# A four-layer transformer chain on one core: 22 expert slots for 20, silu written where the product goes, transposed products over the gathered x, one slot in dead tables and the gate factor

## What is computed

```python
def ec_moe(x, w_router, w_gate, w_up, w_down):
    B, N, _ = x.shape
    cap = CAPACITY_FACTOR * N // N_EXPERTS
    aff = jax.nn.softmax(jnp.einsum('bnd,de->bne', x, w_router).astype(jnp.float32), axis=-1)
    gates, idx = lax.top_k(jnp.swapaxes(aff, 1, 2), cap)
    bidx = jnp.arange(B)[:, None, None]
    xin = x[bidx, idx]
    h = jax.nn.silu(jnp.einsum('becd,edf->becf', xin, w_gate)) * jnp.einsum('becd,edf->becf', xin, w_up)
    out = jnp.einsum('becf,efd->becd', h, w_down) * gates[..., None].astype(x.dtype)
    return jnp.zeros_like(x).at[bidx, idx].add(out.astype(x.dtype))
...
    for i in range(DEPTH):
...
        x = layer_norm(ALPHA * x + h, ln_g[i, 0], ln_b[i, 0])
        y = ec_moe(x, moe_router[i], moe_w_gate[i], moe_w_up[i], moe_w_down[i])
        x = layer_norm(ALPHA * x + y, ln_g[i, 1], ln_b[i, 1])
```

## Time and profile before

| | us |
|---|---|
| median of 3 runs | 1781.36 (1778.82 to 1783.51) |
| the profiled execution | 1783.23 |
| its span on the core | 1780.7 |
| TensorE matmuls busy | 1421.6 |
| TensorE weight loads busy | 928.4 |
| VectorE busy | 601.4 |
| ScalarE busy | 428.1 |
| bytes moved | 533.48 MB, mean 300 GB/s |

### The profile page before, as it was taken

One profiled execution on the slowest core, in us unless ns is written; L12 is line 12 of the kernel. 1 busy time (PEld: TensorE's weight loads), 2 busy tenths in 40 slices (PEclk: granted clock), 3 DMA queues, 4 the chain that ended last, 5 costly groups with the idle time before them and its releaser, 6 DMA issues.

```text
span 1780.7 us, 21467 instructions
## 1 busy us (share of the span) xinstructions
PE 1421.6 (80%) x9010; PEld 928.4 (52%) x9010; DVE 601.4 (34%) x988; ACT 428.1 (24%) x671; POOL 39.3 (2%) x47
## 2 busy tenths in 40 slices
PE   7999765575575799997655755758999999999997
PEld 6788221121121475672211211215999989899996
DVE  5555100000000247651000000002555566865556
ACT  3442100000000233430000000001343454654343
POOL 3000000000000002100000000000000000000000
PEclk9989888777787889998886887869999999999999
DMA  9726999999999952379999999999546665236560
GB/s 338 219 109 273 415 423 424 424 425 423 425 423 424 389 215 95 126 283 424 423 424 424 425 424 424 424 424 386 180 166 197 229 211 166 72 99 205 178 203 24
DMA packets 148836, 533.48 MB, mean 300 GB/s; under 512 B 9868, under 2 KB 73628, under 8 KB 100508
## 3 DMA queue, kind: packets, MB, share of 16 engines
q1 hardware_dynamic: 146148, 527.07, 75.5%
q10 hardware_dynamic: 1176, 2.18, 0.8%
q0 software_dynamic: 1440, 3.18, 0.6%
HBM read 529.78 MB, written 2.62 MB: 299 GB/s over the span
## 4 chain that ended last, share of the span: by engine, by line
PE 52%; DMA 36%; DVE 5%; SPq 4%; ACT 2%; issue 1%; DVEq 0%; ACTq 0%
PE bank L1668 14%; PE bank L613 11%; DMA arena<-in_moe_w_up 9%; DMA moe_slots<-in_moe_w_up 9%; DMA xT<-in_moe_w_down 8%; PE bank L1684 7%; PE bank L1114 5%; DMA moe_slots<-in_moe_w_down 3%; DMA xT<-in_moe_w_up 3%; DMA ring<-in_moe_w_down 3%; PE bank L497 3%; PE bank L1154 3%; PE bank L314 2%; SPq L1308 2%; SPq L1300 1%; DMA ring<-in_moe_w_up 1%
## 5 line engine op out<-in xcount | busy, mean ns | idle before, releaser
L568 DVE TENSOR_TENSOR w_lo<-ring,w_hi 128x1024 fp32r<-128x1024 f32 x200 | 244.4, 1224 | 239.7 <-ACT w_hi L563 232.4
L1114 PE MATMUL bank<-ring,arena 128*32 128x512 f32 x1016 | 217.8, 738 | 99.4 <-DMA ring<-in_moe_w_up 47.9
L563 ACT ACTIVATE w_hi<-ring 128x1024 fp32r<-128x1024 f32 x200 | 211.2, 1058 | 315.9 <-PE bank L1668 151.2
L1668 PE MATMUL bank<-xT_hi,w_hi 128*128 128x256 f32 x704 | 199.8, 284 | 0.6 <-DVE xT_lo L460 0.4
L1668 PE MATMUL bank<-xT_hi,w_lo 128*128 128x256 f32 x704 | 199.2, 283 | 0.0
L1668 PE MATMUL bank<-xT_lo,w_hi 128*128 128x256 f32 x704 | 199.2, 283 | 0.0
L1154 PE MATMUL bank<-ring,arena 128*32 128x512 f32 x536 | 133.9, 815 | 79.0 <-DMA moe_slots<-in_moe_w_down 25.1
L1273 DVE TENSOR_TENSOR arena<-arena,bank 64x512 f32<-64x512 f32 x32 | 22.1, 690 | 433.1 <-ACT arena L1209 433.1
L1114 PEld LDWEIGHTS bank<-ring,arena 128*32 128x32 f32 x1016 | 46.2, 122 | 217.8 <-issue 215.7
L1668 PEld LDWEIGHTS bank<-xT_hi,w_hi 128*128 128x128 f32 x704 | 135.1, 192 | 1.6 <-issue 0.9
L1668 PEld LDWEIGHTS bank<-xT_lo,w_hi 128*128 128x128 f32 x704 | 135.1, 192 | 0.7
(11 more groups left out here) (286 smaller groups left out, 2313.9 us busy)
## 6 DMA issues: line engine op xcount, KB each, us to landing
ring<-in_moe_w_gate SPq DMA_DIRECT2D x76, 1024.0 KB, 26.5
ring<-in_moe_w_down SPq DMA_DIRECT2D x65, 1024.0 KB, 27.0
ring<-in_moe_w_up SPq DMA_DIRECT2D x51, 1024.0 KB, 26.8
arena<-in_moe_w_up SPq DMA_DIRECT2D x28, 1024.0 KB, 26.8
arena<-in_moe_w_gate SPq DMA_DIRECT2D x28, 1024.0 KB, 26.5
moe_slots<-in_moe_w_up SPq DMA_DIRECT2D x24, 1024.0 KB, 26.8
moe_slots<-in_moe_w_gate SPq DMA_DIRECT2D x24, 1024.0 KB, 26.6
moe_slots<-in_moe_w_down SPq DMA_DIRECT2D x24, 1024.0 KB, 27.1
```

The lines of the kernel that those rows point to most:

```text
L563: nc.scalar.activation(dst, raw, ACT.Copy).then_inc(hi_ready, 1)
L568: nc.vector.tensor_tensor(lo, raw, hi.bitcast(F32), ALU.subtract).then_inc(split_ready, 1)
L1114: last = nc.tensor.matmul(ps[B_GU[j % 2]][32 * c:32 * c + 32, :], xin[:, k, j * CAP:(j + 1) * CAP], w, start=(k == 0), stop=(k == KD - 1), ...
L1668: last = nc.tensor.matmul(ps[2 * s + f][:, n * SEQ:(n + 1) * SEQ], w_parts[wp][:, buf, k * P:(k + 1) * P], (xT_hi3, xT_lo3)[xp][:, k, :], ...
```

## The change

- A 21st slot (`SPARE_SLOT`) lies in the arena from column 2816. The room comes from two edits: silu is written to rows 64 to 127 of `hmid`, where the odd expert's product goes, and the tile `silu` is gone; `hT` lies over `xin`, which for that is laid out by expert first (`xin[:, j, k, :]`), so that the copy for experts 0 and 1 overwrites only their gathered x.
- ScalarE's silu of an odd expert waits for VectorE's product of the expert before it. The wait for the last group's scatter moves from VectorE's product and ScalarE's copy to ScalarE's silu of expert 0.
- A 22nd slot (`CONST_SLOT`) consists of two rows of 1024 columns, `cst` from 256 to 1279 and `gk_w`. Its units are loaded by two transfers of 512 KB. It stands behind the fourth load of a layer; it waits for mLSTM's chunk 15 in layer 0 and for GLA's gate product in layer 1. The last 22 units of a layer do without it.
- The memset and the loads of `gk_w` move on GpSimd's queue from the setup to the place between mLSTM and GLA, behind a wait for the last unit of layer 0 in the 22nd slot, and have a counter of their own (`gk_in`), for which TensorE waits ahead of the gate product.

```diff
-NSLOT = 20
+NSLOT = 22
+SPARE_SLOT, CONST_SLOT = 20, 21
...
-        for slots, u in ((ARENA_SLOTS, mixer[11]), (SPLIT_SLOTS, mixer[15]), ((XT_SLOT,), mixer[15])):
+        for slots, u in (((CONST_SLOT,), mixer[8]), ((*ARENA_SLOTS, SPARE_SLOT), mixer[11]), (SPLIT_SLOTS, mixer[15]), ((XT_SLOT,), mixer[15])):
...
-        return self.units(count, range(NSLOT))
+        return self.units(count - NSLOT, range(NSLOT)) + self.units(NSLOT, range(CONST_SLOT))
...
+        spare_at = 2816
+        slots += [arena[:, spare_at:spare_at + SLOT], None]
+        const_rows = (cst[:, C_SEL:C_SEL + D], gk_w[:, :])
...
-        xin = ar(KD * SLOTS_E).rearrange("p (k c) -> p k c", k=KD)
-        silu = ar(2 * HALF).rearrange("p (b n) -> p b n", b=2)
+        xin_hT = ar(KD * SLOTS_E)
+        xin = xin_hT.rearrange("p (j k c) -> p j k c", j=GROUP, k=KD)
+        hT = xin_hT.rearrange("p (b c) -> p b c", b=2)
...
-                                                        xin[:, k, j * CAP:(j + 1) * CAP], w, start=(k == 0),
+                                                        xin[:, j, k, :], w, start=(k == 0),
...
-                    nc.scalar.activation(silu[64:128, j % 2, :], ps[B_GU[j % 2]][0:64, :], ACT.Silu).then_inc(silu_ready, 1)
+                    if j == 0 and g:
+                        act.wait_ge(scattered, n - m)
+                    elif j % 2:
+                        act.wait_ge(h_ready, 4 * n + j)
+                    nc.scalar.activation(hmid[64:128, j // 2, :], ps[B_GU[j % 2]][0:64, :], ACT.Silu).then_inc(silu_ready, 1)
...
-                elif u.slot in ARENA_SLOTS:
+                elif u.slot == CONST_SLOT and m == 0:
+                    sp.wait_ge(const_ready, 2)
+                    sp.wait_ge(chunk_done, ml_mix.done(15))
+                elif u.slot == CONST_SLOT:
+                    sp.wait_ge(ga_psum, 1)
+                elif u.slot in ARENA_SLOTS or u.slot == SPARE_SLOT:
                     sp.wait_ge(z_ready, NT * (m + 1))
...
+            def load(u, src):
+                if u.slot == CONST_SLOT:
+                    for k in range(2):
+                        sp.dma_start(const_rows[k], src[:, k * D:(k + 1) * D]).then_inc(slot_landed[u.slot], 16)
...
             pe.wait_ge(glr_ready, 1)
+            pe.wait_ge(gk_in, 32)
...
+        def gk_gpsimd(pool, link):
+
+            pool.wait_ge(unit_done, max(u.n for u in moe_u[0] if u.slot == CONST_SLOT) + 1)
             link(nc.gpsimd.memset(gk_w[0:2 * RANK, :], 0.0))
...
             ml_gpsimd(pool)
+            gk_gpsimd(pool, link)
             gla_gpsimd(pool)
```

More of the change, by code:

```diff
@@ L132, in unit @@
         s = min(allowed, key=lambda slot: self.last.get(slot, slot - NSLOT))
-        self.landed[s] += 16
+        self.landed[s] += 32 if s == CONST_SLOT else 16
         last = self.last.get(s)
@@ L235, in program, with slot_row @@
         slots += [moe_slots[:, n * SLOT:(n + 1) * SLOT] for n in range(4)] + [xT[:, :]]
+        spare_at = 2816
+        slots += [arena[:, spare_at:spare_at + SLOT], None]
+        const_rows = (cst[:, C_SEL:C_SEL + D], gk_w[:, :])
+        def slot_row(u, k):
+            return const_rows[k] if u.slot == CONST_SLOT else slots[u.slot][:, k * D:(k + 1) * D]
         def slot(u, k):
@@ L1024, in program @@
         pick_gT = ar(NT * P)
-        assert ar.at <= arena_w - 4 * SLOT
+        assert ar.at <= spare_at and spare_at + SLOT <= arena_w - 4 * SLOT
         ar = Arena()
@@ L1203, in moe_scalar @@
                     for k in (2 * part, 2 * part + 1):
-                        ins = nc.scalar.activation(xin[:, k, :], xin_psum(k), ACT.Identity,
+                        ins = nc.scalar.activation(xin[:, :, k, :], xin_psum(k).rearrange("p (j c) -> p j c", j=GROUP), ACT.Identity,
                                                    bias=pair_col(m, 1, k), scale=pair_col(m, 0, k))
@@ L1265, in moe_vector @@
                     for k in (2 * part, 2 * part + 1):
[L1266 removed]
+                        ins = nc.vector.tensor_scalar(xin[:, :, k, :], xin_psum(k).rearrange("p (j c) -> p j c", j=GROUP), pair_col(m, 0, k), pair_col(m, 1, k),
                                                       ALU.mult, ALU.add)
@@ L1270, in moe_vector @@
                     dve.wait_ge(silu_ready, 4 * n + j + 1)
-                    if j == 0 and g:
-                        dve.wait_ge(scattered, n - m)
-                    nc.vector.tensor_tensor(hmid[64 * (j % 2):64 * (j % 2) + 64, j // 2, :], silu[64:128, j % 2, :],
+                    nc.vector.tensor_tensor(hmid[64 * (j % 2):64 * (j % 2) + 64, j // 2, :], hmid[64:128, j // 2, :],
                                             ps[B_GU[j % 2]][64:128, :], ALU.mult).then_inc(h_ready, 1)
@@ L1290, in wait_slot @@
                     sp.wait_ge(xT_taken, m + 1)
+            def load(u, src):
+                if u.slot == CONST_SLOT:
+                    for k in range(2):
+                        sp.dma_start(const_rows[k], src[:, k * D:(k + 1) * D]).then_inc(slot_landed[u.slot], 16)
+                else:
+                    sp.dma_start(slots[u.slot], src).then_inc(slot_landed[u.slot], 16)
             for g in range(NGROUP):
@@ L1299, in moe_sync @@
                             src = a[name][m, g * GROUP + j].rearrange("(q p k) f -> p q (k f)", p=P, k=2)
-                            sp.dma_start(slots[u.slot], src[:, part, :]).then_inc(slot_landed[u.slot], 16)
+                            load(u, src[:, part, :])
                 for q in range(KD // 2):
@@ L1306, in moe_sync @@
                         src = a["moe_w_down"][m, g * GROUP + j].rearrange("(q p k) d -> p q k d", p=P, k=2)
-                        cols = slice(0, HALF if tail else D)
-                        sp.dma_start(slot(u, 2)[:, :, cols], src[:, q, :, cols]).then_inc(slot_landed[u.slot], 16)
+                        if tail:
+                            sp.dma_start(slot(u, 2)[:, :, 0:HALF], src[:, q, :, 0:HALF]).then_inc(slot_landed[u.slot], 16)
+                        else:
+                            load(u, src[:, q].rearrange("p k d -> p (k d)"))
                     if tail:
```

12 lines of the change are left out of this document (5 added, 7 removed).

## The result

The changed kernel takes 1770.79 us (median of 13 runs, 1767.57 to 1776.79); the kernel before, run beside it, 1781.13 us (13 runs, 1776.14 to 1783.51). The ratio of the two is **0.9959, 95% interval 0.9947 to 0.9971**, which is 7.3 us less (5.2 to 9.4). The two medians lie 10.3 us apart, the means 7.7. The executions of the changed kernel fall into two clusters, seven from 1767.57 to 1770.79 and six from 1775.51 to 1776.79, and its median is the last of the lower one. Those of the kernel before spread from 1776.14 to 1783.51. So a median can jump by some 5 us on one execution, and the ratio with its interval is the better number. One execution of run x9 (1832.11 us) and one of x4 (2515.31) were in a slower state of the chip and stand in no ratio. The profiled execution took 1770.46 us, with a span of 1768.6.

The account below looks back on a forecast made before the run. The expert layers were taken as bound by their weight stream, 424 GB/s or 2.47 us a unit. From 1781.36 us, -9.89 for two slots and +1.1 for short rows, -8.8 in all, gave 1772.6 us, range 1769.0 to 1777.8.

Parts of the forecast that it names:

- What bounds the layers: Both expert layers: weight stream without gaps at 424 GB/s, 2.47 us a unit, from the first reuse of a slot on.
- -9.89 us for two slots: Both expert layers: 22 units instead of 20 loaded by the restart, 4.94 us less in each.
- The cover ahead of the restart: Before each layer's first slot reuse: the two extra loads fit into holes of the transfers and cost nothing.
- The price of a constants unit, +0.08: Expert streams: 14 units with 4 KB rows take 2.55 us each, +1.1 us in all; ends 0 and +5.5.
- The gate factor: GpSimd, behind unit 158 of layer 0 at about 527 us: over 100 us of slack, cost 0.
- The ends of the layers: Last 22 units: gla units 7 to 9 wait for the last down products; 6 us of slack stay.
- The restart stays.: First reuse of a slot in each layer: depends on routing and gather, not slots; near 177.4 us in layer 0.
- the forecasts for 604, 794.6 and 1221.4 us: Layer 0's last landing (before 608.5), layer 1's first slot reuse, and layer 1's last landing (before 1230.2).
- 4 KB rows at +0.39: Rival, constants units in the stream: rows cost what they cost alone, +5.5 in place of +1.1, 1777.0 us; 13%.
- The extra loads aren't hidden: Rival, ahead of the layers: added loads delay the prefetch or a slot brings nothing, 1776.4 or 1781.4 us; 6%.
- A fixed cost for each transfer: Rival, the 14 extra transfers in the stream: 2.3 us more each, +32.6, 1804 us; 4%.
- The gate factor late: Rival, GLA's gate product: loads land past some 635 us, whole gain lost past 644; 2%.

Follow-up runs that it names:

- x9: The changed kernel again, unedited, as a second profiled execution: ratio 0.9949 to the kernel before.
- x4: Kernel before with each 1 MB load cut into two of 64 partitions, rows still 8 KB: median 2491.02 us, ratio 1.3956.
- x1: Changed kernel with the constants slot used once a layer, ahead of the restart, never in the stream: ratio 0.9948 to the kernel before.
- x10: Repeat on another chip of the changed kernel with the constants slot used once a layer: 1769.54 us, ratio 0.9939 to the kernel before.
- x7: Changed kernel with 20 slots, neither new slot used, gate factor loaded in the setup, layout and moved waits kept: ratio 1.0011 to the kernel before.
- x3: Kernel before with each 1 MB expert load issued as two loads with rows of 4 KB: ratio 1.0125.
- x6: Kernel before with each 1 MB expert load kept as one load but with rows of 4 KB (other output, same work): ratio 1.0124.
- x2: Changed kernel with 21 slots, constants slot unused and gate factor loaded in the setup: ratio 0.9968 to the kernel before.

## Why the prediction was right

1772.6 us was forecast, 1770.8 measured, within the range; -8.8 us forecast, -7.3 (5.2 to 9.4) by the ratio and -6.7 by the two streams. The mechanism is right. That the measured median lies below the forecast is luck: the median is the last execution of the lower cluster, and the next one is at 1775.5, above the forecast and still in the range. By its steps:

- **What bounds the layers.** Right, and the strongest point: from 18 over 20 to 21 slots the stream falls by 2.4 to 2.5 us for each, and by 2.1 to 2.6 us for the 22nd where it takes no unit in the stream (x1, x10), at an unchanged rate of 423 to 424 GB/s.
- **-9.89 us for two slots.** Right: x1 has 4.5 and 4.8 us less a layer, x10 4.6 and 5.0, together 9.3 and 9.6. What is missing is in layer 0, where the gate factor's loads pass.
- **The cover ahead of the restart.** Right. Between the load of xT and the restart lie 8.0 us (163.57 to 171.58; 7.3 before, and 9.6 in x7, which has none of the added loads), and the added loads are not waited for.
- **The price of a constants unit, +0.08.** The step that was mis-sized. The price of the rows is right, 0.06 to 0.07 by x3 and x6. But 14 x 0.08 = 1.1 stood for all that the slot costs in the stream, and that is 2.5 us: the first reuse behind the restart costs 0.6 to 0.7 us in each layer, the twelve others 0.10 each. The forecast took the price of a full queue for all 14 units, and for the first the queue is short; whether that is the reason is not shown.
- **silu in place, xin by expert, moved waits.** Cost 0, right (x7).
- **The gate factor.** Right that nothing waits for it: GpSimd's memset starts at 522.65 us, forecast 527 (the restart is 5.8 us earlier), the loads have landed at 530.1, and the product that reads them starts at 631.3. But its price in the stream was put too low: 0.15 us forecast, some 0.6 by the rate while its loads pass.
- **The ends of the layers.** "No wait of SyncE at gla unit 7" was wrong in its words: SyncE waits 5.6 us for down products there in two pieces. But it waited 4.7 in two before, and from the last pass to GLA's first product it is 13.81 us in both. It costs nothing.
- **"The restart stays."** Nothing speaks against it for the mean over executions, since the ratio's 7.3 us are the 6.7 of the streams within the interval. In one execution it does not stay: it moves by up to 7.5 us, in step with the clock (170.29 to 177.80 in the table), and the forecasts for 604, 794.6 and 1221.4 us could be held against the trace only as lengths.

The rivals: *4 KB rows at +0.39* fell with x3 and x6 (0.06 to 0.07). *The extra loads aren't hidden* fell with x1 and x2. *A fixed cost for each transfer* fell with x3: 336 added transfers cost at most 0.01 us each beyond their short rows. The Trainium skill, page "DMA: Bandwidth & Descriptors", section Bandwidth, has the rule to make transfers of at least 1 MiB. It did not bind in this full queue: halves of 512 KB over all partitions ran at 414 GB/s, and a single load with the same rows at 414 too. *The gate factor late* did not happen.

## What to carry to other kernels

In a phase that is bound by a transfer stream, as here, buffers were worth what they held at its start and no more. Count the units that have landed when the first buffer comes back, and leave a poor buffer (short rows, two transfers) out of the rotation afterwards. If a load of a full stream must be split, split it by columns: by partitions it cost half the rate here. A small load from another queue that passes in the stream costs more than its bytes. And read a change of half a percent by the lengths of its phases, since the phase that TensorE bounds moved by several us from one execution to the next.

## What the runs showed of the hardware

- Loads of 64 partitions with 8 KB rows, two in place of one of 128, move 227 GB/s in a full queue where the whole loads move 424, at the same busy share of the 16 engines (1.02 and 1.01).
- Rows of 4 KB move 414 GB/s, of 8 KB 424, and one load or two of them make no difference in the rate.
- Two loads of 32 KB from GpSimd's queue beside the full stream lower the rate to 379 GB/s for 4 us (the change and x1), a loss of some 0.6 us for 0.15 us of bytes.
- One kernel, two executions on two chips (x1, x10): TensorE's granted clock from 100 to 125 us is 0.78 in the one and 0.93 in the other, and the expert layer's first reuse of a slot is 5.6 us apart. The streams behind it agree within 0.2 us.
